# Second block of a two-block network: half of the value projection moved between the index steps, and a top-k selection cut into single rounds

## The reference, cut to what matters

```
for l in range(2):
    h = rmsnorm(x, norm_g[l])
    q, k, v, ga, iq, ik, iw, xr, gr, ma, mb = split(h @ w_in[l])
    q, k, iq, ik = rope(q), rope(k), rope(iq), rope(ik)
    # index: 16 heads of 64; the 64 best keys of every query are kept
    score = sum_h iw[h] * relu(iq[h] @ ik.T);  keep = top_k(causal(score), 64)
    y_a = (softmax(q @ k.T over keep) @ v * silu(ga)) @ w_out_attn
    hr  = rg_lru(conv4(xr))                    # recurrence over time, 16 blocks of 88
    y_b = (hr * silu(gr)) @ w_out_rnn
    x = x + (sigmoid(ma) * y_a + sigmoid(mb) * y_b) @ w_o
out = rmsnorm(x, final_g)
```

## Time and profile before

| | us |
|---|---|
| median of 3 runs | 2351.17 (2344.51 to 2351.41) |
| profiled execution, its own time | 2350.82 |
| its span, first to last instruction | 2349.0 |
| mean granted TensorE clock | 0.977 |
| second block, layer 0 | 1565 to about 1953 of the span |
| second block, layer 1 | about 1953 to 2349 |

### The profile page before, as it was taken

The page is one execution under the profiler, slowest core; times in us unless marked ns, Lnnn a source line. Parts: engine busy times, 40 slices in busy tenths (PEclk is TensorE's granted clock), DMA queues, the critical chain, the costliest instruction groups (busy, mean ns, idle before and its releaser), DMA issues.

```text
span 2349.0 us, 34405 instructions
## 1 busy us (share of the span) xinstructions
PE 2237.4 (95%) x13903; PEld 1967.3 (84%) x13903; DVE 1695.4 (72%) x2152; ACT 1420.0 (60%) x1894; POOL 318.9 (14%) x314
## 2 busy tenths in 40 slices
PE   7889999988999999999999999969998999998998
PEld 7778999867888888888888888859997988988897
DVE  5633655778999998999898989954689335478724
ACT  5432444556777777777777877845565514555722
POOL 0510000000000000000000000005545101653400
PEclk9898999998999999999999999979999999999999
DMA  9422656427999999999999999937545356753443
GB/s 251 129 73 73 233 181 184 167 71 255 341 344 388 363 348 362 355 354 365 351 357 353 367 349 363 346 115 224 163 129 161 121 182 186 214 160 115 154 122 106
DMA packets 328397, 556.42 MB, mean 237 GB/s; under 512 B 23616, under 2 KB 164680, under 8 KB 328232
## 3 DMA queue, kind: packets, MB, share of 16 engines
q1 hardware_dynamic: 318432, 527.63, 64.4%
q0 software_dynamic: 9120, 25.97, 4.6%
q10 hardware_dynamic: 680, 0.54, 0.1%
HBM read 544.12 MB, written 9.96 MB: 236 GB/s over the span
## 4 chain that ended last, share of the span: by engine, by line
PE 79%; DVE 12%; ACT 6%; issue 2%; POOL 1%; DMA 0%; SPq 0%; ACTq 0%; DVEq 0%; POOLq 0%
PE bank L864 22%; PE bank L866 21%; PE bank L865 21%; PE bank L905 6%; DVE parts L2438 3%; ACT parts L1818 2%; PE bank L870 1%; PE bank L1533 1%; PE bank L1019 1%; DVE fast L2438 1%; ACT work L2375 1%; PE bank L1594 1%; POOL work L728 1%; DVE work L3209 1%; ACT bank L2366 1%
## 5 line engine op out<-in xcount | busy, mean ns | idle before, releaser
L2438 DVE TENSOR_TENSOR parts<-raw,parts 128x1024 fp32r<-128x1024 f32 x665 | 809.6, 1232 | 378.8 <-ACT parts L1818 355.9
L1818 ACT CAST parts<-raw 128x1024 fp32r<-128x1024 f32 x665 | 692.0, 1047 | 479.7 <-PE bank L866 466.2
L864 PE MATMUL bank<-cols,parts 128*128 128x256 f32 x1680 | 498.9, 297 | 9.2 <-DVE parts L2438 5.8
L866 PE MATMUL bank<-cols,parts 128*128 128x256 f32 x1680 | 479.8, 286 | 1.3 <-issue 1.3
L865 PE MATMUL bank<-cols,parts 128*128 128x256 f32 x1680 | 480.1, 286 | 0.0
L2438 DVE TENSOR_TENSOR fast<-raw,fast 128x1024 fp32r<-128x1024 f32 x302 | 361.9, 1218 | 33.5 <-ACT fast L1818 16.2
L1818 ACT CAST fast<-raw 128x1024 fp32r<-128x1024 f32 x302 | 315.8, 1052 | 95.5 <-PE bank L866 88.7
L864 PEld LDWEIGHTS bank<-cols,parts 128*128 128x128 f32 x1680 | 327.5, 195 | 23.3 <-issue 19.5
L865 PEld LDWEIGHTS bank<-cols,parts 128*128 128x128 f32 x1680 | 327.5, 195 | 6.7 <-issue 5.8
L866 PEld LDWEIGHTS bank<-cols,parts 128*128 128x128 f32 x1680 | 327.0, 195 | 0.0
L864 PE MATMUL bank<-parts,cols 128*128 128x512 f32 x740 | 294.9, 399 | 13.6 <-DVE parts L2438 6.9
(11 more groups left out here) (376 smaller groups left out, 3249.4 us busy)
## 6 DMA issues: line engine op xcount, KB each, us to landing
raw<-in_moe_w_gate_dram SPq DMA_DIRECT2D x112, 1024.0 KB, 5.9
raw<-in_moe_w_up_dram SPq DMA_DIRECT2D x112, 1024.0 KB, 5.9
raw<-in_moe_w_down_dram SPq DMA_DIRECT2D x112, 1024.0 KB, 6.2
raw<-in_w_in_dram SPq DMA_DIRECT2D x76, 1024.0 KB, 5.5
raw<-in_a_w_in_dram SPq DMA_DIRECT2D x12, 1024.0 KB, 12.9
raw<-in_ffn_w_gate_dram SPq DMA_DIRECT2D x11, 1024.0 KB, 5.2
raw<-in_ffn_w_up_dram SPq DMA_DIRECT2D x11, 1024.0 KB, 5.2
raw<-in_ffn_w_down_dram SPq DMA_DIRECT2D x11, 1024.0 KB, 4.9
```

The costliest lines, as they stand in the source:

```text
L864: pe.matmul(o, l[0], r[0], start=start, stop=False)
L866: return pe.matmul(o, l[1], r[0], start=False, stop=stop)
L1818: a.copy(dst[0], src).then_inc(*up(o + "hi", x))
L2438: v.tensor_tensor(dst[1], src, dst[0].bitcast(F32), ALU.subtract).then_inc(*up(o + "lo", x))
```

## The change: what it does

The four pieces of `v1` are projected behind iq instead of behind xr, and SP's table follows. Each of the four gets one index step behind it, and every second one a step of the recurrence. The single recurrence step behind the old v1 goes, and iq gives one such step (behind its fourth pair) instead of two. The index generators get four steps more: DVE yields behind each of the eight rounds, not behind every second. Some banks are renumbered: iq uses (0, 1, 2, 3), q and k use (2, 3, 0, 1).

```diff
--- before.py
+++ after.py
@@ -617,12 +617,12 @@
         wv = w[:, :].rearrange("(k p) c -> p k c", p=128)
         t["v0"] = rm_table(w, O_V, 512)
         t["xr"] = fm_table(w, O_XR, 11)
-        t["v1"] = rm_table(w, O_V + 512, 512)
         x, = W.chunk((8, 128), [(at_cols(64 * i, 64), wv[:, :, O_IK:O_IK + 64]) for i in range(2)], [whole])
         W.used(x)
         t["ik"] = x
         t["iw"] = narrow_table(wv[:, :, O_IW:O_IW + 16], 16)
         t["iq"] = fm_table(w, O_IQ, 8)
+        t["v1"] = rm_table(w, O_V + 512, 512)
         t["q"] = fm_table(w, O_Q, 8)
         t["k"] = fm_table(w, O_K, 8)
         t["ga"] = fm_table(w, O_GA, 8)
@@ -910,7 +910,7 @@
                 busy[b] = (*ev, i)
                 tick(ticks - ticks // 2)
 
-        def rm(blocks, xt, banks, ev, ticks=0, c0=0):
+        def rm(blocks, xt, banks, ev, ticks=0, c0=0, each=0, also=None):
 
             for c, mine in enumerate(blocks, c0):
                 for q, x in enumerate(mine):
@@ -923,6 +923,9 @@
                                 claim(banks[t])
                             k_ = mm3(bank[banks[t]][:, :], sl(xt, ALL, k, slice(t * 128, (t + 1) * 128)), sl(w, ALL, i), k == 0, k == 7)
                     k_.then_inc(*up("used", x))
+                    tick(each)
+                    if also and q % 2:
+                        next(also, None)
                 for t in range(2):
                     busy[banks[t]] = (*ev, c, t)
                     tick(ticks)
@@ -1706,7 +1709,7 @@
                         nr += 2
                         yield
                         yield
-                for r in range(5):
+                for r in range(9):
                     yield
 
             def qk2(u, q, o, l=l):
@@ -1748,8 +1751,6 @@
             rm_first(t_["v0"][0], XT, (0, 1), (("h", l),), ("v", l, 0), lambda l=l: h_cols(l, 1))
             lane.back[:] = [rn]
             fm(t_["xr"], XT, (2, 3, 0, 1), ("xr", l))
-            rm(t_["v1"], XT, (0, 1), ("v", l), c0=1)
-            tick()
             x = t_["ik"]
             _, w = piece_view(W, x)
             pe.wait_ge(*at("lo", x))
@@ -1759,10 +1760,11 @@
             k_.then_inc(*up("used", x))
             narrow(bank[4][:, T:T + 64], t_["iw"], 16, 4)
             busy[4] = ("iw", l)
-            fm(t_["iq"], XT, (2, 3, 0, 1), ("iq", l), pace=lambda nb: nb % 2)
+            fm(t_["iq"], XT, (0, 1, 2, 3), ("iq", l), pace=lambda nb: nb // 3)
             lane.back[:] = [ix]
-            fm(t_["q"], XT, (0, 1, 2, 3), ("q", l), ticks=2, also=rn)
-            fm(t_["k"], XT, (0, 1, 2, 3), ("k", l), ticks=2, also=rn)
+            rm(t_["v1"], XT, (0, 1), ("v", l), c0=1, each=1, also=rn)
+            fm(t_["q"], XT, (2, 3, 0, 1), ("q", l), ticks=2, also=rn)
+            fm(t_["k"], XT, (2, 3, 0, 1), ("k", l), ticks=2, also=rn)
             fm(t_["ga"], XT, (0, 1, 2, 3), ("ga", l), ticks=2, also=rn)
             lane.finish(ix)
             lane.back[:] = [at_]
@@ -1842,10 +1844,13 @@
                     after(("c", c))
                 tick(ticks - ticks // 2)
 
-        def rm(blocks, evac, ticks=0, c0=0):
+        def rm(blocks, evac, ticks=0, c0=0, each=0, also=None):
             for c, mine in enumerate(blocks, c0):
-                for x in mine:
+                for q, x in enumerate(mine):
                     after(x)
+                    tick(each)
+                    if also and q % 2:
+                        next(also, None)
                 for t in range(2):
                     evac(t, c, mine[-1])
                     tick(ticks)
@@ -2386,17 +2391,16 @@
             rm(t_["v0"], v_evac)
             lane.back[:] = [rn]
             fm(t_["xr"], to(L2.GR, "xr", 2))
-            rm(t_["v1"], v_evac, c0=1)
-            tick()
             after(t_["ik"])
             after(t_["iw"])
             a.wait_ge(*at("used", t_["iw"]))
             a.copy(L2.IK, bank[4][:, 0:T]).then_inc(*up("ik", l))
             a.mul(L2.iw2, bank[4][:, T:T + 64], 0.03125).then_inc(*up("iw", l))
-            fm(t_["iq"], to(L2.IQ, "iq", 2), pace=lambda nb: nb % 2)
+            fm(t_["iq"], to(L2.IQ, "iq"), pace=lambda nb: nb // 3)
             lane.back[:] = [ix]
-            fm(t_["q"], to(L2.QT, "q"), ticks=2, also=rn)
-            fm(t_["k"], to(L2.KT, "k"), ticks=2, also=rn)
+            rm(t_["v1"], v_evac, c0=1, each=1, also=rn)
+            fm(t_["q"], to(L2.QT, "q", 2), ticks=2, also=rn)
+            fm(t_["k"], to(L2.KT, "k", 2), ticks=2, also=rn)
             fm(t_["ga"], tanh_to(L2.GA, "ga_th", 4), ticks=2, also=rn)
             lane.finish(ix)
             lane.back[:] = [at_]
@@ -2464,10 +2468,13 @@
                     after(("c", c))
                 tick(ticks - ticks // 2)
 
-        def rm(blocks, ticks=0, c0=0):
+        def rm(blocks, ticks=0, c0=0, each=0, also=None):
             for c, mine in enumerate(blocks, c0):
-                for x in mine:
+                for q, x in enumerate(mine):
                     after(x)
+                    tick(each)
+                    if also and q % 2:
+                        next(also, None)
                 for t in range(2):
                     tick(ticks)
 
@@ -3207,8 +3214,7 @@
                     v.wait_ge(*at("dve"))
                     for n, sc in ((0, s0), (1, s1)):
                         v.match_replace(sc, L2.m8[:, n, :], sc, -3.0e38).then_inc(*up("dve"))
-                    if r % 2:
-                        yield
+                    yield
                 for n, sc in ((0, s0), (1, s1)):
                     v.wait_ge(*at("dve"))
                     v.tensor_scalar(sc, sc, -2.0e38, None, ALU.is_lt).then_inc(*up("dve"))
@@ -3273,12 +3279,11 @@
             rm(t_["v0"])
             lane.back[:] = [rn]
             fm(t_["xr"], None)
-            rm(t_["v1"], c0=1)
-            tick()
             after(t_["ik"])
             after(t_["iw"])
-            fm(t_["iq"], None, pace=lambda nb: nb % 2)
+            fm(t_["iq"], None, pace=lambda nb: nb // 3)
             lane.back[:] = [ix]
+            rm(t_["v1"], c0=1, each=1, also=rn)
             fm(t_["q"], None, ticks=2, also=rn)
             fm(t_["k"], None, ticks=2, also=rn)
             fm(t_["ga"], silu(L2.GA, "ga", 4), ticks=2, also=rn)
```

## The result

| | before | after |
|---|---|---|
| median, us (6 runs each) | 2347.96 (2344.51 to 2351.41) | 2335.71 (2333.04 to 2340.62) |
| ratio of the runs, 95% interval | | 0.995 [0.9934, 0.9966] |
| profiled execution, span | 2350.82, 2349.0 | 2334.00, 2332.2 |

The account below looks back on a forecast made before the run. PE's matmul stream was taken as the floor, with only its waits winnable, chiefly on DVE's backlog from ga. Per layer 6.8 - 0.8 - 0.6 = 5.4 us, twice 10.8, off 2350.8 gave 2340.0 us; range 2333 to 2349.

Parts of the forecast that it names:

- What bounds the kernel: Whole kernel: PE's matmuls are the floor; the large winnable wait, 7.2 us a layer, is a DVE backlog arising in ga.
- The relief in ga: In ga: three weighings (4.5 us), the masking (1.3) and one selection round (1.4) leave DVE's stretch, together 7.2 us.
- The wait at the third rotation: At the third attention rotation: PE's wait for DVE to read the bank falls from 7.2 to 0.5 us.
- The cover in k: In k: net 3 us added to DVE, taken at 0 because DVE idled 4.66 us ahead of ga; otherwise 3.
- What is late next: At the seventh attention rotation: PE meets DVE again, with 1.7 us of new waits.
- 6.8 us won a layer: Attention rotations: the seventh starts at 1778.1 against 1784.89, and this gain is carried to the end of the layer.
- Around v1: From the end of iq to q: 0.8 us lost a layer at index step 7, 0.6 to POOL's taps.
- Sum: Whole kernel: 6.8 - 0.8 - 0.6 = 5.4 us won a layer, twice 10.8, giving 2340.0 us.

Follow-up runs that it names:

- the second series: The unaltered changed kernel timed again beside the kernel before: 2335.93 against 2344.72 us, ratio 0.9958 [0.9942, 0.9974].

## Why the prediction was right

- **What bounds the kernel.** Right. The one large wait was a DVE backlog of ga: less selection shrinks it nearly one for one, finer steps alone don't.
- **The relief in ga, 7.2 us of DVE.** The stretch from the opening conversion to the one at rotation 1 was to take 26.6 us and takes 27.0 (1726.91 to 1753.94).
- **The wait at the third rotation, 0.5 us.** Mis-sized: 1.77. DVE stood at rotation 1 8.65 us behind PE (1746.43 to 1755.08), where 7.5 was forecast. 0.4 us is the longer stretch. The three weighings that left were costed by their duration, 1.51 us, where the distance between rows is 1.42; the mask, now beside POOL, took 2.15 us (1751.79 to 1753.94) for 1.58 before, and a conversion 2.24 for 2.07; single rounds, 1.31 us each for 1.38, gave 0.4 back. 0.7 is the entry to ga: I let ACT's block hold DVE there and gave back half a us for a relu. The opening conversion now stands without any idle time ahead of it, so DVE itself was late.
- **The cover in k.** Priced at 0, and nearly so. The 4.66 us of idle time are used up to the last: the weighings that moved into k met POOL's taps of pair 4 and took 2.95 and 2.75 us instead of the 1.51 of the earlier trace rows. What I costed from a row held only while POOL was quiet.
- **What is late next.** Right in place and, in layer 0, in price: DVE paces PE from the third to the seventh rotation, 16.9 us (1755.81 to 1772.74) against the 16.7 read off before, with a wait of 1.54 us at the seventh in layer 0 (1.7 forecast). In layer 1 0.19 us is left, because PE ran slower there behind the 1.75 us wait.
- **6.8 us won a layer from rotation 1 to 7.** 5.3 and 6.0. I carried the 6.8 to the end of the layer; up to the attention proper 5.2 are left in both layers. In layer 1 most of the rest goes into the wait there for DVE, 0.77 us where it was 0.18.
- **Around v1, 1.4 us lost a layer.** 2.1 and 1.1. `roped` came 29.0 us behind the end of iq (28.2 forecast) and step 7 waits 1.83 us (2.2). The 0.8 between are POOL's: without full taps the wait is 1.04 us. The extra us in layer 0 is PE at a lower clock behind that wait: its eight dot products take 1.57 us against 1.06 in layer 1, and the distance to the next ones is 8.5 us at a granted clock of 0.80 against 7.0 at 1.00; layer 1 loses 0.46 of that to a wait for ACT. I hadn't priced that the four pieces of v1, once interrupted, take 12.2 us instead of 10.9.
- **Sum: 5.4 us a layer.** Measured on the changed stretches: 3.0 and 4.0. The forecast of 10.8 us met a median difference of 12.2 (8.8 in the second series) with the help of unchanged stretches, which the prediction didn't have. The mechanism was right; its size was 3.7 us too large, and the total came out well partly by luck. The absolute time was off by 4.3 us (2340.0 against 2335.71), of which 2.9 are the base: the forecast starts from the profiled execution, 2350.8, and the median of all six runs before was 2347.96.

That the selection's single rounds matter at all was not in the prediction, which gave no price to cutting them. They do, by a way of their own: they let `run(3)` through in time for PE's pair 4.

By the Trainium skill, "SBUF — State Buffer", "Who interferes with whom", two-input VectorE operations and GpSimd operations that read SBUF lock each other out. The measurements agree in direction: both engines' busy times grew with the overlap, and the weighing went from 566 to 376 ns when the taps were cut.

## What to carry to other kernels

When PE waits for a buffer that a slower engine should long have read, sum that engine's work from its last idle moment to the read: what leaves this stretch counts nearly one for one (4.7 to 4.8 us for 5.5 here) unless PE's own work leaves with it, what is only reshuffled in it counts for nothing, unless something behind it in the queue is wanted earlier by someone else. Moving work costs at both ends: price it beside its new neighbours, POOL above all, not by its row in the old place. And compare the unchanged stretches of two traces before crediting a change with the whole difference.

## What the runs showed of the hardware

- Two engines lengthen each other's work: with the same instructions, DVE was busy 9.3 us and POOL 8.2 us longer after the change, and DVE 24 us less with short taps.
- PE's clock behind a pause: after a 7.2 us wait the 24 matmuls and the rotation took 5.59 us instead of 3.73, at a granted clock of 0.66 (6.33 us and 0.56 in layer 1). After a wait of 1.8 us it differs: 3.95 us at 1.00 in layer 0, 5.42 us at 0.69 in layer 1 (2138.97 to 2144.39), in both profiles of the changed kernel. The length of the wait alone doesn't say what it costs behind it. Two stretches of the kernel before and two of the changed kernel (us, PE busy, granted clock, DMA share, GB/s):

```profile
1768.10:1773.70 5.60, 5.58 (x26) 0.66 0.62 190
2155.50:2161.80 6.30, 6.28 (x26) 0.56 0.54 169
```

```profile
1755.80:1759.70 3.90, 3.89 (x26) 1.00 0.92 285
2138.90:2144.40 5.50, 5.42 (x27) 0.69 0.88 249
```

- Unchanged matmuls at the head of layer 0 took 23.0 us in both profiles of the changed kernel and 25.9 in both of the kernel before; the other kernels show 25.1 to 26.0. What in a kernel sets this stays open: the programs with 23.0 and 25.2 us (the changed kernel and the one with rounds in pairs) have the same instructions up to that point.
- The clock can also fall with no idle time of PE, during or behind the 32 narrow matmuls of `iw` (0.51 from 1635.30 to 1638.70 in the kernel before): the 192 matmuls of iq took 25.15 us in the kernel with rounds in pairs and 23.12 in the changed kernel, again with the same instructions up to there.
